# Forgetting attention's scores on a Trainium2 core: the order of 64-row products, 128-row bias products and one small copy

## Chip, core and metric

One NeuronCore of one Trainium2 chip runs the whole program. The metric is device time in microseconds (us) from one launch; three runs of the kernel before gave 2244.13, 2245.39 and 2246.12 us, so the median is 2245.39 us. Lower is better.

## What is computed

The reference runs two transformer blocks over 256 tokens of width 1024, each with attention to a 256-token memory and a mixture of experts. The second block begins with a hybrid mixer, and one of its three parts is the forgetting attention (4 heads of width 64), cut here to what matters:

```python
cum = jnp.cumsum(log_f, axis=-1)                     # log_f = log_sigmoid(ff + fox_fb), per head
logits = jnp.einsum('bhqd,bhkd->bhqk', q_blk, k).astype(jnp.float32) * scale
logits = logits + c_blk[..., :, None] - cum[..., None, :]
logits = jnp.where(key_pos[None, :] <= q_pos[:, None], logits, -jnp.inf)
p = jax.nn.softmax(logits, axis=-1).astype(v.dtype)
return jnp.einsum('bhqk,bhkd->bhqd', p, v)
```

## The kernel before

The kernel is written engine by engine, with semaphores set by hand, so that the order of the code is the order on each queue. TensorE (PE) does every product; VectorE (DVE) and ScalarE (ACT) split float32 weights into a high and a low part (`w_high`, `w_low`), and a product of weights is three matmuls (lines 809 to 811: high by high, low by high, high by low). ACT makes a high part (line 1449) and DVE the low part (`lows`, line 1923, one half-panel each); SyncE (SP) loads weight panels into three ring slots (line 469), and a slot is free when DVE has split its panel.

The mixer's projections stand on PE in the order `fqk` (queries and keys of the forgetting attention), `fv`, `hf`, `dqk`, `dv`, `hq`, `hi`, `hg`. After the first half of `hf` PE makes the running sums of the forget gates (`fox_sums`, lines 1179 to 1181), waits until DVE has copied them out of the PSUM bank that the scores will take (`small_read`, line 2566), and makes the scores (`fox_scores`). The second half of `hf`, the first half of `dqk`, and the turning of the probabilities (`turn_map(1)`, lines 1219 to 1221) follow.

A score tile is 128 queries by 128 keys (`tc` = 0, the first half of the queries) or by 256 keys (`tc` = 1). Per head it is a product of q by k over 64 rows of the array (line 1193 or 1197; rows 0 to 63 for heads 0 and 2, rows 64 to 127 for heads 1 and 3) and, accumulated onto it, the bias by products over all 128 rows: the log forget gates, broadcast, by a triangle of ones (`upto`) or by ones (line 1194, or lines 1198 to 1200). The heads go in the order 0, 2, 1, 3, and two heads share a PSUM bank: places 0 and 1 (heads 0 and 2) in bank 4 or 5, places 2 and 3 (heads 1 and 3) in bank 7 or 6. All these operands are float32, and each such matmul is two passes in the trace ("x2").

When a `tc` is done PE signals `map_scores`; DVE adds the query's own sum and the mask (line 2572), takes maxima (2002, 2003), splits the second half of `dqk` (1923), and normalises (2009, 2010) what ACT has exponentiated (1468). PE's `turn_map(1)` waits for that (`probs_ready`). The differential attention later makes its scores over 32 rows of the array in the same head order (line 1209), four 128-column and four 256-column products at a time with nothing between them; `diagonals` (line 1250) is eight 128-row, 128-column float32 products in a row.

Of the kernel before, what the change touches and what calls it, by code (L numbers as in the profile page):

```python
# [21 lines left out]
P = 128  # L22
T = 256
# [19 lines left out]
HEAD_ORDER = (0, 2, 1, 3)  # L43
# [155 lines left out]
def program(nc, ins, const_in, out):  # L199
    ctx = ExitStack()  # L200
    with ctx:
# [5 lines left out]
        def S(name):  # L207
            if name not in sems:
                sems[name] = ctx.enter_context(nc.semaphore(name))
            return sems[name]  # L210
# [21 lines left out]
        ps = ctx.enter_context(nc.psum_tensor("ps", [P, 8, 512], F32))  # L232

        def c_(name):

            a, n = CONST_COLS[name]
            if a >= RESIDENT:
                return ring[:, 6, a - RESIDENT:a - RESIDENT + n]
            return const[:, a:a + n]

        def w_(off, *shape):
            n = int(np.prod(shape))
            v = work[:, off:off + n]
            if len(shape) == 2:
                return v.rearrange("p (a b) -> p a b", b=shape[1])
            if len(shape) == 3:
                return v.rearrange("p (a b c) -> p a b c", b=shape[1], c=shape[2])
            return v
# [12 lines left out]
        def vec(name, r=0):  # L261
            a = VEC_AT[name] + r
            return cols[:, a:a + 1]

        IDENT, ONES = c_("ident"), c_("ones")
        FQK, DQK, QH, KH = w_(0, 4, T), w_(1024, 4, T), w_(2048, 4, T), w_(3072, 4, T)
# [69 lines left out]
        for u in range(len(UNITS) + 1):  # L336
# [15 lines left out]
            weight, layer, c0, n, columns, src = UNITS[u]  # L352
# [44 lines left out]
        def half_tile(q, parts):  # L397

            t, (_, kind, _, n) = parts[:, q % SPLITS, :], pieces_split[q]
            if kind == "rows":  # L400
                return t
            if kind == "features":
                return t.rearrange("p (k n) -> p k n", n=PANEL)[:, :, 0:n]
            if q in range(ffn_at, ffn_at + 3 * FFN_TURNS):
                return t.rearrange("p (k g n) -> p k g n", g=2, n=P)
            return t.rearrange("p (k n) -> p k n", n=T)

        def halves_to(name, more=0):

            return split_at[UNIT[name]] + 2 + more  # L410
# [222 lines left out]
        def _(pe):  # L633
            mm = nc.tensor.matmul
# [52 lines left out]
            def evicted(name):  # L687
                u = UNIT[name]
                pe.wait_ge(S(f"unit_read{u % 2}"), u // 2 + 1)
# [208 lines left out]
            for t in range(VEC_TILES):  # L898
                n = min(P, VEC_ROWS - t * P)
                last = nc.tensor.transpose(ps[:, 0, t * P:t * P + n], w_(0, VEC_TILES, P)[0:n, t, :], IDENT[0:n, 0:n])  # L900
# [7 lines left out]
            for g in range(4):  # L908
                last = mm(ps[:, 4 + g // 2, g % 2 * T:g % 2 * T + T], poolw[:, g, :], w_(0, 4, T)[:, g, :],
                          start=True, stop=True)  # L910
# [84 lines left out]
            for b in range(TAPS_ON_PE):  # L995
                for k in range(CONV):
# [3 lines left out]
                       start=(k == 0), stop=(k == CONV - 1)).then_inc(S("diagonal_used"), 1)  # L1000
# [7 lines left out]
            for kc in range(KC):  # L1008
# [4 lines left out]
                last = mm(ps[:, 7, 0:T], ONES, SQ[:, kc, :], start=(kc == 0), stop=(kc == KC - 1))  # L1013
# [161 lines left out]
            upto, ones = c_("upto"), ONES  # L1175
# [7 lines left out]
            def fox_scores():  # L1183

                evicted("fqk")
                for tc in range(2):
                    for place, h in enumerate(HEAD_ORDER):
                        p0 = 64 * (h % 2)
                        first, second = (minus_logf[:, i, h:h + 1].broadcast_to([P, P]) for i in range(2))
                        q = FQK[p0:p0 + 64, h // 2, tc * P:(tc + 1) * P]  # L1190
                        if tc == 0:
                            o = ps[:, 4 + 3 * (place // 2), place % 2 * P:place % 2 * P + P]
                            mm(o, q, FQK[p0:p0 + 64, 2 + h // 2, 0:P], start=True, stop=False)
                            last = mm(o, first, upto, start=False, stop=True)
                        else:
                            o = ps[:, 5 + place // 2, place % 2 * T:place % 2 * T + T]
                            mm(o, q, FQK[p0:p0 + 64, 2 + h // 2, :], start=True, stop=False)
                            mm(o[:, 0:P], first, upto, start=False, stop=False)
                            mm(o[:, P:T], first, ones, start=False, stop=False)
                            last = mm(o[:, P:T], second, upto, start=False, stop=True)  # L1200
                    last.then_inc(S("map_scores"), 1)

            def diff_scores(which):
# [121 lines left out]
            for h in range(4):  # L1325
# [3 lines left out]
                last = mm(ps[:, 5, h * P:(h + 1) * P], CR[:, h, :], v(0), start=False, stop=True)  # L1329
# [507 lines left out]
        def _(dve):  # L1837
# [80 lines left out]
            def lows(end):  # L1918

                while n_["halves"] < end:  # L1920
                    q = n_["halves"]
                    dve.wait_ge(S("parts_high"), q + 1)
                    V.tensor_tensor(half_tile(q, w_low), half_source(q), half_tile(q, w_high).bitcast(F32), SUB)\  # L1923
                        .then_inc(S("parts_split"), 1)
                    n_["halves"] += 1
# [38 lines left out]
            def row(b):  # L1964
                n_[f"b{b}"] += 1
                dve.wait_ge(S(f"brow{b}_loaded"), 16 * n_[f"b{b}"])
                return brow[:, b, :]
# [50 lines left out]
            def map_scores(tc):  # L2018
                if tc == 0:
                    return ps[:, 4:8:3, 0:T].rearrange("p a (b t) -> p a b t", t=P)  # L2020
                return ps[:, 5:7, :].rearrange("p a (b t) -> p a b t", t=T)
# [93 lines left out]
            for k in range(3):  # L2115
                for b in range(4):
                    wv = vec("ev_conv_a", 4 * k + b)
                    if k == 0:
                        last = V.tensor_scalar(CT[:, b, :], AP_[:, b, 0:T], wv, None, MUL)
                    else:  # L2120
                        last = V.scalar_tensor_tensor(CT[:, b, :], AP_[:, b, k:k + T], wv, CT[:, b, :], MUL, ADD)
# [4 lines left out]
            for g, win in enumerate(WINDOWS):  # L2126

                cur, size, nxt = UP[:, g, :], 1, SA
                while size < win:
                    n = 272 - 2 * size  # L2130
# [4 lines left out]
                last = V.tensor_tensor(PO[:, g, :], PO[:, g, :], UP[:, g, 8:264], SUB)  # L2135
# [9 lines left out]
            for g in range(4):  # L2145
                if g % 2 == 0:
                    n_["act"] += 1
                    dve.wait_ge(S("columns_by_act"), n_["act"])
                last = V.scalar_tensor_tensor(XT_low[:, 4 + g, :], ps[:, 4 + g // 2, g % 2 * T:g % 2 * T + T], vec("ev_pool_scale", g),
                                              XT_high[:, 4 + g, :].bitcast(F32), MUL, SUB)  # L2150
# [20 lines left out]
            for e, raw in ((8, router1), (16, router)):  # L2171
# [3 lines left out]
                last = V.tensor_tensor(both[:, :, e:2 * e], raw, both[:, :, 0:e].bitcast(F32), SUB)  # L2175
# [53 lines left out]
            for j in range(2):  # L2229
# [17 lines left out]
                for b in range(4):  # L2247
                    last = V.scalar_tensor_tensor(inner[:, b, :], inner[:, b, :], vec("od_pw1_b", 4 * j + b),
                                                  w_(2304, 4, T)[:, b, :], ADD, MUL)
# [6 lines left out]
            for k in range(CONV):  # L2256
                for kc in range(KC - TAPS_ON_PE):
                    wv = vec("od_dw_w", KC * k + kc)
                    if k == 0:
                        last = V.tensor_scalar(CO[:, kc, :], HC[:, kc, 0:T], wv, vec("od_dw_b", kc), MUL, ADD)  # L2260
                    else:
                        last = V.scalar_tensor_tensor(CO[:, kc, :], HC[:, kc, k:k + T], wv, CO[:, kc, :], MUL, ADD)  # L2262
# [17 lines left out]
            for kc in range(KC):  # L2280
# [3 lines left out]
                last = V.tensor_tensor(XT_low[:, kc, :], SQ[:, kc, :], XT_high[:, kc, :].bitcast(F32), SUB)  # L2284
# [3 lines left out]
            b = row(0)  # L2288
# [225 lines left out]
            for tc in range(2):  # L2514
                last = V.tensor_tensor_reduce(out=scaled[:, tc, :], in0=H[:, tc, :], in1=g, scale=1.0, scalar=0.0, op0=MUL, op1=ADD,
                                              accum_out=mean[:, tc:tc + 1])
# [8 lines left out]
            for tc in range(2):  # L2525
                last = V.scalar_tensor_tensor(centred[:, tc, :], scaled[:, tc, :], mean[:, tc:tc + 1], g, ADD, MUL)
# [5 lines left out]
            for tc in range(2):  # L2532
                last = V.scalar_tensor_tensor(H[:, tc, :], centred[:, tc, :], rstd[:, tc:tc + 1], w_(11264, D), MUL, ADD)
# [25 lines left out]
            dve.wait_ge(S("fox_logits"), 1)  # L2559
            step(V.tensor_tensor(logf_fox, logf_fox, ffa, SUB))  # L2560
            V.tensor_scalar(minus_logf, logf_fox, -1.0, None, MUL).then_inc(S("fox_log"), 1)
            lows(halves_to("dqk", -1))

            cs = ffa
            dve.wait_ge(S("fox_sums"), 1)
            V.tensor_copy(cs, ps[:, 7, 496:504].rearrange("p (a e) -> p a e", e=4)).then_inc(S("small_read"), 1)
            dve.wait_ge(S("small_read"), 1)
            masks = row(0).rearrange("p (k a t) -> p k a t", k=2, a=2)
            for tc in range(2):
                dve.wait_ge(S("map_scores"), tc + 1)  # L2570
                for place, h in enumerate(HEAD_ORDER):
                    last = V.scalar_tensor_tensor(MAPS[1][tc][:, place, :], map_scores(tc)[:, place // 2, place % 2, :], cs[:, tc, h:h + 1],
                                                  masks[:, 0, tc, 0:(tc + 1) * P], ADD, ADD)
# [39 lines left out]
            first, second = w_(8192, 12 * P), w_(9728, 12 * P)  # L2613
# [125 lines left out]
            for tc in range(2):  # L2739
                last = V.scalar_tensor_tensor(centred[:, tc, :], XS[:, tc, :], mean[:, tc:tc + 1], g, ADD, MUL)  # L2740
# [4 lines left out]
            b = row(1 - gain_row[0])  # L2745
# [27 lines left out]
```

## Time and profile before

| what | value |
|---|---|
| runs | 2244.13, 2245.39, 2246.12 us; median 2245.39 |
| profiled execution's own span | 2245.6 us |
| PE busy | 2184.1 us, 97% of the span |
| DVE busy | 1726.1 us, 77% |
| ACT busy | 1363.6 us, 61% |
| mean granted TensorE clock | 0.987 of full |

The page lists for each engine the time in which it was busy. A granted clock (PEclk) of 1.00 is 2.4 GHz, one of 0.50 is 1.2 GHz. The span is from the first instruction to the last of the one profiled execution; it is 0.2 us over the median of the runs.

### The profile page before, as it was taken

How to read it: one execution, taken by the hardware profiler on the slowest of the kernel's cores; microseconds unless marked ns; L12 is line 12 of the kernel's file. 1: busy time of each engine (PE TensorE's matmuls, PEld its weight loads, DVE VectorE, ACT ScalarE, POOL GpSimd, SP SyncE). 2: the span in 40 equal slices, each digit the busy share in tenths (PEclk: the TensorE clock that was granted, in tenths of full speed). 3: DMA queues.
4: the chain of work that ended last, by engine and by line, in shares of the span. 5: the costliest groups of instructions: out<-in, count | busy, mean ns of one | idle time of the engine just before them, and what ended most of it. 6: DMA issues, size and time to landing. Idle time of an engine off the chain costs nothing. (4 is left out here: it accounts for less than half of the span.)

```text
span 2245.6 us, 30564 instructions
## 1 busy us (share of the span) xinstructions
PE 2184.1 (97%) x11743; PEld 1872.3 (83%) x11743; DVE 1726.1 (77%) x1614; ACT 1363.6 (61%) x1205; POOL 83.4 (4%) x79
## 2 busy tenths in 40 slices
PE   7999999999999999999999999999899999999997
PEld 7998999968878888888888888888689988788886
DVE  4755555698568888888888888888756665698897
ACT  4454333427457777777777777777546344477775
POOL 3000000000000000000000000000000000000000
PEclk9999999999999999999999999999889999999999
DMA  9542555532279999999999999999634251799995
GB/s 301 186 160 94 193 200 193 183 113 82 78 282 383 375 386 376 380 375 382 375 381 380 375 390 367 383 366 396 254 130 160 76 200 63 247 365 380 375 379 228
DMA packets 274825, 617.26 MB, mean 275 GB/s; under 512 B 9537, under 2 KB 34321, under 8 KB 274737
## 3 DMA queue, kind: packets, MB, share of 16 engines
q1 hardware_dynamic: 265648, 584.43, 71.1%
q0 software_dynamic: 9088, 31.60, 4.6%
q8 instruction: 62, 1.02, 0.2%
q14 instruction: 27, 0.21, 0.0%
HBM read 603.41 MB, written 12.58 MB: 274 GB/s over the span
## 5 line engine op out<-in xcount | busy, mean ns | idle before, releaser
L2464 DVE TENSOR_TENSOR w_low<-ring,w_high 128x2048 fp32r<-128x2048 f32 x426 | 971.3, 2290 | 134.6 <-ACT w_high L1730 134.0
L1730 ACT ACTIVATE w_high<-ring 128x2048 fp32r<-128x2048 f32 x426 | 815.2, 1917 | 169.1 <-PE ps L811 169.1
L810 PE MATMUL ps<-w_high,parts 128*128 128x512 f32 (+2 forms) x1896 | 736.5, 388 | 0.0
L809 PE MATMUL ps<-w_high,parts 128*128 128x512 f32 x1560 | 617.8, 396 | 4.8 <-DVE gates L2368 3.4
L811 PE MATMUL ps<-w_low,parts 128*128 128x512 f32 x1560 | 609.0, 390 | 0.0
L810 PEld LDWEIGHTS ps<-w_high,parts 128*128 128x128 f32 x1896 | 357.5, 189 | 69.4
L1923 DVE TENSOR_TENSOR w_low<-ring,w_high 128x2048 fp32r<-128x2048 f32 (+2 forms) x117 | 262.2, 2253 | 115.2 <-ACT w_high L1449 109.0
L809 PEld LDWEIGHTS ps<-w_high,parts 128*128 128x128 f32 x1560 | 293.3, 188 | 66.7 <-DVE gates L2368 3.8
L811 PEld LDWEIGHTS ps<-w_low,parts 128*128 128x128 f32 x1560 | 293.3, 188 | 62.7
L1449 ACT ACTIVATE w_high<-ring 128x2048 fp32r<-128x2048 f32 (+2 forms) x117 | 219.7, 1884 | 147.3 <-PE ps L811 127.1
L809 PE MATMUL ps<-XT_high,w_high 128*128 128x256 f32 x1024 | 293.4, 287 | 7.0 <-DVE parts L1914 5.2
L810 PE MATMUL ps<-XT_high,w_low 128*128 128x256 f32 x1024 | 290.7, 284 | 0.0
L811 PE MATMUL ps<-parts,w_high 128*128 128x256 f32 x1024 | 290.6, 284 | 0.0
L809 PE MATMUL ps<-w_high,XT_high 128*128 128x512 f32 (+2 forms) x592 | 232.5, 393 | 2.7 <-DVE parts L2284 1.3
L811 PE MATMUL ps<-w_low,XT_high 128*128 128x512 f32 (+2 forms) x592 | 228.3, 386 | 0.0
L809 PEld LDWEIGHTS ps<-XT_high,w_high 128*128 128x128 f32 x1024 | 197.4, 193 | 10.7 <-issue 8.1
L810 PEld LDWEIGHTS ps<-XT_high,w_low 128*128 128x128 f32 x1024 | 197.4, 193 | 0.7
L811 PEld LDWEIGHTS ps<-parts,w_high 128*128 128x128 f32 x1024 | 197.4, 193 | 0.0
L809 PEld LDWEIGHTS ps<-w_high,XT_high 128*128 128x128 f32 x592 | 111.8, 189 | 25.6 <-issue 3.9
L811 PEld LDWEIGHTS ps<-w_low,XT_high 128*128 128x128 f32 x592 | 111.6, 189 | 22.8
L810 PE MATMUL ps<-w_high,XT_high 128*128 128x512 f32 x256 | 99.6, 389 | 0.0
L2262 DVE SCALAR_TENSOR_TENSOR work<-work,cols 128x256 f32<-128x256 f32 x180 | 74.0, 480 | 1.1
(445 smaller groups left out, 1661.7 us busy)
## 6 DMA issues: line engine op xcount, KB each, us to landing
ring<-in_od_moe_gu SPq DMA_DIRECT2D x224, 1024.0 KB, 8.2
ring<-in_od_moe_down SPq DMA_DIRECT2D x112, 1024.0 KB, 7.6
ring<-in_w SPq DMA_DIRECT2D x96, 1024.0 KB, 8.6
ring<-in_ev_ffn_gu SPq DMA_DIRECT2D x22, 1024.0 KB, 7.7
ring<-in_xa_wkv SPq DMA_DIRECT2D x8, 2048.0 KB, 8.2
ring<-in_od_pw_w SPq DMA_DIRECT2D x6, 2048.0 KB, 8.4
ring<-in_w_in SPq DMA_DIRECT2D x6, 2048.0 KB, 7.9
ring<-in_ev_ffn_down SPq DMA_DIRECT2D x11, 1024.0 KB, 5.1
```

The lines of the kernel that those rows point to most:

```text
L809: mm(out_, xh, wh, start=start, stop=False)
L810: mm(out_, xl, wh, start=False, stop=False)
L811: return mm(out_, xh, wl, start=False, stop=stop)
L1449: A(half_tile(q, w_high), half_source(q), ACT.Copy).then_inc(S("parts_high"), 1)
L1730: A(w_high[:, j % SPLITS, :], ring[:, j % NS, :], ACT.Copy).then_inc(moe_sem(k, "high"), 1)
L1923: V.tensor_tensor(half_tile(q, w_low), half_source(q), half_tile(q, w_high).bitcast(F32), SUB)\
L2262: last = V.scalar_tensor_tensor(CO[:, kc, :], HC[:, kc, k:k + T], wv, CO[:, kc, :], MUL, ADD)
L2464: V.tensor_tensor(w_low[:, j % SPLITS, :], ring[:, j % NS, :], w_high[:, j % SPLITS, :].bitcast(F32), SUB)\
```

## The change

In `fox_scores` the four 64-row products of a `tc` are issued together, and the 128-row bias products of all four heads behind them. A bank's first product carries `start`, the bank's second goes without it, and the checks on groups are skipped. On DVE the copy of the sums, with PE's permission that follows from it, stands ahead of the low part of `dqk`'s first half, no longer behind it. Numbers of instructions, their sizes and operands stay.

```diff
 evicted("fqk")
 for tc in range(2):
+    n = (tc + 1) * P
+    places = [ps[:, 4 + 3 * a if tc == 0 else 5 + a, b * n:(b + 1) * n] for a in range(2) for b in range(2)]
     for place, h in enumerate(HEAD_ORDER):
         p0 = 64 * (h % 2)
+        mm(places[place], FQK[p0:p0 + 64, h // 2, tc * P:(tc + 1) * P], FQK[p0:p0 + 64, 2 + h // 2, 0:n],
+           start=(place % 2 == 0), stop=False, skip_group_check=True)
+    for place, h in enumerate(HEAD_ORDER):
+        o = places[place]
         first, second = (minus_logf[:, i, h:h + 1].broadcast_to([P, P]) for i in range(2))
-        q = FQK[p0:p0 + 64, h // 2, tc * P:(tc + 1) * P]
-        if tc == 0:
-            o = ps[:, 4 + 3 * (place // 2), place % 2 * P:place % 2 * P + P]
-            mm(o, q, FQK[p0:p0 + 64, 2 + h // 2, 0:P], start=True, stop=False)
-            last = mm(o, first, upto, start=False, stop=True)
-        else:
-            o = ps[:, 5 + place // 2, place % 2 * T:place % 2 * T + T]
-            mm(o, q, FQK[p0:p0 + 64, 2 + h // 2, :], start=True, stop=False)
-            mm(o[:, 0:P], first, upto, start=False, stop=False)
-            mm(o[:, P:T], first, ones, start=False, stop=False)
-            last = mm(o[:, P:T], second, upto, start=False, stop=True)
+        last = mm(o[:, 0:P], first, upto, start=False, stop=(tc == 0), skip_group_check=True)
+        if tc == 1:
+            mm(o[:, P:T], first, ones, start=False, stop=False, skip_group_check=True)
+            last = mm(o[:, P:T], second, upto, start=False, stop=True, skip_group_check=True)
     last.then_inc(S("map_scores"), 1)
...
 V.tensor_scalar(minus_logf, logf_fox, -1.0, None, MUL).then_inc(S("fox_log"), 1)
-lows(halves_to("dqk", -1))

 cs = ffa
 dve.wait_ge(S("fox_sums"), 1)
 V.tensor_copy(cs, ps[:, 7, 496:504].rearrange("p (a e) -> p a e", e=4)).then_inc(S("small_read"), 1)
 dve.wait_ge(S("small_read"), 1)
+lows(halves_to("dqk", -1))
```

PE before, from the last of the sums through the scores of `tc` = 0 and one head of `tc` = 1 (the second matmul operand's columns close each row):

```order
L1181 MATMUL ps<-small,const 128x4
L1193 MATMUL ps<-work 128x128 [waits unit_read0,small_read]
L1194 MATMUL ps<-const,small 128x128
L1193 MATMUL ps<-work 128x128
L1194 MATMUL ps<-const,small 128x128
...
L1197 MATMUL ps<-work 128x256
L1198 MATMUL ps<-const,small 128x128
L1199 MATMUL ps<-const,small 128x128
L1200 MATMUL ps<-const,small 128x128
L1197 MATMUL ps<-work 128x256
```

The same place on PE with the change (L1191 is the 64-row product, L1196 to L1199 the bias; the rows of the last three heads' bias, which repeat these, are left out):

```order
L1181 MATMUL ps<-small,const 128x4
L1191 MATMUL ps<-work 128x128 [waits unit_read0,small_read]
L1191 MATMUL ps<-work 128x128 x3
L1196 MATMUL ps<-const,small 128x128 x4
L1191 MATMUL ps<-work 128x256 x4
L1196 MATMUL ps<-const,small 128x128
L1198 MATMUL ps<-const,small 128x128
L1199 MATMUL ps<-const,small 128x128
```

Before, each head changes from 64 rows to 128 rows and back; with the change there are one block of 64-row and one of 128-row products for each `tc`.

DVE before, from the gates' logarithms to the first additions onto the scores:

```order
L2561 TENSOR_SCALAR small<-small 128x8 [waits vector_step]
L1923 TENSOR_TENSOR w_low<-ring,w_high 128x2048 [waits parts_high]
L2566 COPY small<-ps 128x8 [waits fox_sums]
L2572 SCALAR_TENSOR_TENSOR work<-ps,small,brow 128x128 [waits map_scores,brow0_loaded,small_read]
L2572 SCALAR_TENSOR_TENSOR work<-ps,small,brow 128x128 x3
```

DVE with the change, same place:

```order
L2560 TENSOR_SCALAR small<-small 128x8 [waits vector_step]
L2564 COPY small<-ps 128x8 [waits fox_sums]
L1922 TENSOR_TENSOR w_low<-ring,w_high 128x2048 [waits parts_high,small_read]
L2571 SCALAR_TENSOR_TENSOR work<-ps,small,brow 128x128 [waits map_scores,brow0_loaded]
L2571 SCALAR_TENSOR_TENSOR work<-ps,small,brow 128x128 x3
```

The copy has moved ahead of one low part, which is now held until the sums are there.

## Rows read from the trace of the kernel before

**Rows 1.** The page's busy times, shares of the span.

```profile
PE 2184.1 (97%) x11743; PEld 1872.3 (83%) x11743; DVE 1726.1 (77%) x1614; ACT 1363.6 (61%) x1205; POOL 83.4 (4%) x79
```

**Rows 2.** PE's waits from 1700 us to the end; total us, times, longest.

```profile
PE ps L809 <- DVE gates L2368: 1.8, 1, 1.8
...
PE ps L674 <- DVE XS L2688: 0.4, 1, 0.4
PE ps L1105 <- DVE XS L2410: 0.3, 1, 0.3
```

**Rows 3.** PE's timeline at the scores: start us, us, instruction, [idle before <-releaser].

```profile
1661.73 0.36 PE L1181 MATMUL ps<-small,const 128*128 128x4 f32 x2
1663.33 0.48 PE L1193 MATMUL ps<-work 64*128 64x128 f32 x2 [1.23 <-DVE small L2566]
1663.75 0.49 PE L1194 MATMUL ps<-const,small 128*128 128x128 f32 x2
...
1666.06 0.79 PE L1193 MATMUL ps<-work 64*128 64x128 f32 x2
1666.79 0.79 PE L1194 MATMUL ps<-const,small 128*128 128x128 f32 x2
...
1669.25 0.63 PE L1199 MATMUL ps<-const,small 128*128 128x128 f32 x2
1669.67 0.63 PE L1200 MATMUL ps<-const,small 128*128 128x128 f32 x2
...
1678.14 0.77 PE L809 MATMUL ps<-w_high,XT_high 128*128 128x512 f32 x1
```

**Rows 4.** PE's timeline at line 1250, eight 128-row float32 products in a row.

```profile
1728.69 2.02 PE L1250 MATMUL ps<-work 128*128 128x128 f32 x16
1730.47 0.48 PE L809 MATMUL ps<-w_high,XT_high 128*128 128x512 f32 x1
```

**Rows 5.** Busy us and granted clock (PEclk) of stretches around the scores.

```profile
1661.40:1665.50 4.10, 2.87 (x18) 2.17 (x16) 1.88 (x2) 3.19 (x2) 0.00 (x0) 1.00 1.03 393
1668.60:1678.10 9.50, 9.50 (x31) 6.82 (x31) 0.24 (x1) 0.00 (x0) 0.00 (x0) 0.50 0.00 0
1678.10:1682.60 4.50, 4.50 (x13) 3.53 (x13) 3.90 (x9) 1.38 (x7) 0.00 (x0) 0.50 0.00 0
1682.60:1685.80 3.20, 3.20 (x16) 2.61 (x15) 3.06 (x5) 2.24 (x10) 0.00 (x0) 1.00 0.05 3
```

**Rows 6.** PE's timeline: start and end of `hf`'s first half, end of its second.

```profile
1655.89 0.40 PE L809 MATMUL ps<-w_high,XT_high 128*128 128x512 f32 x1
...
1661.37 0.28 PE L1179 MATMUL ps<-small,const 128*128 128x4 f32 x2
...
1685.79 0.28 PE L809 MATMUL ps<-XT_high,w_high 128*128 128x256 f32 x1
```

**Rows 7.** DVE's timeline from the log gates to the first additions.

```profile
1659.37 0.17 DVE L2561 TENSOR_SCALAR small<-small 128x8 f32<-128x8 f32 x1
1660.91 2.29 DVE L1923 TENSOR_TENSOR w_low<-ring,w_high 128x2048 fp32r<-128x2048 f32 x1 [1.37 <-ACT w_high L1449]
1663.12 0.16 DVE L2566 COPY small<-ps 128x8 f32<-128x8 f32 x1
1667.72 1.12 DVE L2572 SCALAR_TENSOR_TENSOR work<-ps,small,brow 128x128 f32<-128x128 f32 x4 [4.44 <-PE ps L1194]
```

**Rows 8.** PE's timeline at line 1209, 32-row products of the differential attention.

```profile
1715.51 1.68 PE L1209 MATMUL ps<-work 32*128 32x128 f32 x16
1717.12 0.38 PE L809 MATMUL ps<-XT_high,w_high 128*128 128x256 f32 x1
```

**Rows 9.** Timeline behind the scores: DVE's additions and normalising, PE's turning.

```profile
1678.60 1.66 DVE L2572 SCALAR_TENSOR_TENSOR work<-ps,small,brow 128x256 f32<-128x256 f32 x4 [9.75 <-PE ps L1200]
...
1685.71 1.22 DVE L2010 TENSOR_TENSOR work<-work,small 128x1024 f32<-128x1024 f32 x1
...
1691.55 0.27 PE L1219 MATMUL ps<-const,work 128*128 128x128 f32 x1
```

**Rows 10.** Other stretches: busy us of PE, PEld, DVE, ACT, POOL, then PEclk.

```profile
1774.80:1778.20 3.40, 2.14 (x20) 2.00 (x19) 3.37 (x5) 3.35 (x4) 0.00 (x0) 0.99 0.02 5
1778.20:1785.00 6.80, 6.80 (x34) 6.80 (x34) 5.60 (x9) 1.06 (x2) 0.00 (x0) 0.50 0.07 8
1787.80:1791.90 4.10, 2.90 (x18) 2.39 (x18) 2.68 (x6) 1.21 (x4) 0.00 (x0) 1.00 0.69 260
1955.70:1959.10 3.40, 3.40 (x9) 2.64 (x8) 0.78 (x2) 0.50 (x1) 1.84 (x1) 0.50 1.04 364
```

## The prediction

> **What bounds the kernel now.** I read the page's busy times first: PE is busy for 97% of the span and DVE for 77% [rows 1], so the question is what PE loses at the place of the change, and whether a gain there is kept. The waits of PE behind that place come next: the list has ten kinds, none on a DMA, the longest 1.8 us, and all on DVE or ACT work that PE itself feeds [rows 2]. So PE sets the end, and what it gains at the scores should arrive at the end nearly whole.
>
> Then PE's timeline at the scores. The reader is to see three losses. PE stands idle for 1.23 us before the first product, until DVE's copy [rows 3]. Then a 64-row product and a 128-row product alternate, start to start 0.42 us, where eight 128-row products of that size without such a change take 1.78 us, 0.22 us each [rows 3, 4]. And the spacing grows: from 1666.06 it is 0.73 us for the same alternation, because the granted clock, 1.00 up to about 1665.5, is 0.50 (1.2 GHz instead of 2.4) from there to 1682.6, past the end of the scores and well into `hf`'s second half [rows 3, 5]. The scores take from 1663.33 to 1678.14, 14.81 us [rows 3], and `hf`'s second half from there to 1685.79, 7.65 us, where its first half, as large, took 5.48 us from 1655.89 to 1661.37 [rows 3, 6].
>
> **The wait for the copy.** DVE has nothing to do from 1659.54 to 1660.91, then makes `dqk`'s low part for 2.29 us, and copies the sums only at 1663.12 [rows 7]; PE had them ready at 1661.73 + 0.36 = 1662.09 [rows 3]. With the copy first, DVE starts it 0.14 us after PE's end (as at line 2572: 1666.79 + 0.79 = 1667.58, started 1667.72 [rows 3, 7]), takes 0.16, and PE starts 0.05 later (1663.28 to 1663.33). That is 1662.44: a gain of **0.9 us**. The low part then runs from about 1662.4 to 1664.7 where it ended at 1663.2. It is queued ahead of the additions of `tc` = 0, which could start at about 1664.2, so these are held by 0.5 us; the additions of `tc` = 1 wait for PE till after 1668 in any case. PE needs that low part only when `dqk` begins, behind all of `hf`. So moving it costs nothing. If the cover went, it would cost at most those 0.5 us.
>
> **The changes between 64 and 128 rows.** A change costs 0.42 - 0.22 = 0.20 us at full clock, and 0.73 - 0.42 = 0.31 at half, the 0.42 being lines 1199 to 1200 at half clock [rows 3, 4]. Among the scores there are 15 such changes, 7 within each `tc` and one between; with the edit 3 are left. Twelve go: **2.4 us** at full clock.
>
> **The 64-row products side by side.** No row shows 64-row products in sequence. The nearest is line 1209: four 128-column and four 256-column products over 32 rows, same head order, same banks. Its 16 passes and the change to what follows take 1717.12 - 1715.51 = 1.61 us [rows 8]. One behind another they would take 4 x 0.22 + 4 x 0.43 = 2.6 us and 0.2 for the change, so half of them ran beside the others: two heads lie in one part of the array's rows and two in another. The forgetting heads lie likewise in rows 0 to 63 and 64 to 127, and the two parts write different banks. The bounds are no pairing (2.6 us, gain nothing) and full pairing (1.4 us): **1.2 us**, of which I take all, by that row.
>
> **The clock.** The scores after, at full clock: 1.61 for the 64-row blocks, 16 bias products at 0.22 = 3.56, two more changes 0.4: 5.6 us. The scores before would be 2.6 + 3.56 + 15 x 0.20 = 9.2 us at full clock, against 14.8 measured; so the low clock costs 5.6 us there, and 7.65 - 5.48 = 2.2 us in `hf`: 7.8 us in all. Does it still fall? Before it fell, PE was busy for 2.87 of 4.10 us, and most products had a change ahead of them [rows 5]. The busy share alone does not tell: PE was busy for 2.90 of 4.10 us at 1787.8 and the clock stayed at 1.00, and it fell after 2.14 of 3.40 us at 1774.8 [rows 10]. The same stretch of the changed kernel has 0.35 us of idle time (1662.09 to 1662.44) and two changes, so some 0.9 busy; that lies on the side of the stretches that kept it. I take the clock as held: **7.8 us**, bounds 0 and 7.8.
>
> The Trainium skill has a rule on weight loads that speaks against packing the bias products: by "TensorE: Matmul & The Clock Gate", Part 3, The mechanism, a weight load overlaps running matmuls only when the row group differs, which would leave every pass of a block of 128-row products with its load in the open. The trace does not bear it out: 16 passes, each with its own load, started in 1.78 us [rows 4].
>
> **The sum.** 0.9 + 2.4 + 1.2 + 7.8 = 12.3 us. Checked the other way: from 1662.44, 5.6 for the scores and 5.5 for `hf`'s second half end at 1673.5 instead of 1685.79. Downstream, DVE's chain from the additions of `tc` = 1 to the normalised maps took from 1678.60 to 1686.93 = 8.3 us, and PE turned them at 1691.55, 4.6 us later [rows 9]. After: scores done 1668.0, chain done 1676.5, PE there at 1668.0 + 5.5 + 5.76 (`dqk`, 1685.79 to 1691.55) = 1679.3; 2.8 us to spare. What is late next is this chain, not yet binding. Profiled span 2245.6 - 12.3 = 2233.3; the span stands 0.2 over the median of the runs, so **2233.1 us**.
>
> **Rivals.** *The clock falls all the same* (0.19). It is the largest term, and other stretches show it falls at shares not far off [rows 10]. If it fell at 1665.5 as before, 2.5 us of full-clock work would take 5, and `hf` would lose up to the 2.2 us that it loses now: 4.7 us given back, 2237.8. The short low stretches elsewhere, 3.4 and 6.8 us [rows 10], would cost half their length, 1.7 or 3.4. I put this case at 2236.0.
>
> *The 64-row products run one behind another* (0.05): the edit then saves only changes, and 1.2 us stay: 2234.3. Against it: the 32-row products [rows 8]; for it: these were 32 rows, not 64.
>
> *Weight loads of the bias products in the open* (0.02): every one of 32 passes costs about 0.21 us, as a first pass after a change does, not 0.11: 3.2 us back, 2236.3. This is the rule of the page named above, and the block of 128-row products is against it [rows 4].
>
> *The chain on DVE and ACT takes over* (0.04): the turning waits for the probabilities. It decides once the chain is 2.8 us later than worked out; a chain as long as the 4.4 us wait it would replace gives 2235 to 2237. For it: DVE now makes a low part between sums and additions. Against: DVE waited 4.44 and 9.75 us for PE there [rows 7, 9].
>
> *Slower* (0.02): the block of 64-row products leaves the clock low, and `hf` and `dqk` do not bring it back. Low clock costs half of its length, so the gains of 12.3 us are gone once it is low for some 25 us from 1662.4, to about 1687 on the new time axis, beyond the turning; each further 2 us costs 1, and low until 1693 gives 2248. Against it: full-size products brought the clock back within 4.5 us here [rows 5].
>
> **How the numbers follow.** About 0.2% (4.5 us) is what a measurement of this kernel can tell from no change. The forecast has 0.68. All cases but the last, and a small part of the clock and chain cases together (0.03), gain over 4.5 us: faster 0.95, same 0.03, slower 0.02. The range takes the forecast's own scatter, since other low stretches later (3.4 and 6.8 us [rows 10]) can shrink, go or grow as PE arrives earlier, 1.7 us each way for one: 2230.5 at the low end. The high end takes in no pairing and all but the worst of the fallen clock: 2237.5.
>
> **What would show each step.** Right: PE's wait before line 1191 about 0.3 us; 16 passes of line 1191 in pairs; a gap of 0.2 us at only three changes; PEclk 1.00 from 1662 through `hf`; first `dqk` product near 1673.5; `turn_map` without a wait. Wrong: PEclk 0.50 anywhere between 1665 and 1675, spacing of 0.21 us and not 0.11 between passes of line 1191 or 1196, or a wait of line 1219 on DVE line 2009.

## The result and the profile after

The changed kernel took 2231.59 to 2233.53 us in four runs, median **2232.7**, against 2242.99 to 2246.12 us, median 2244.76, for the kernel before beside it: a ratio of 0.9946 with a 95% interval of 0.9934 to 0.9958, some 12 us. The forecast was 2233.1 us, in a range of 2230.5 to 2237.5. One run below, of the kernel with the wait filled, was in a slow state (2429.9 us, granted clock 0.849) and enters no figure.

The page's busy times, as [rows 1]: PE is busy for 13.9 us less, the other engines for as long as before.

```profile
span 2230.7 us, 30565 instructions
PE 2170.2 (97%) x11743; PEld 1862.7 (84%) x11743; DVE 1726.2 (77%) x1614; ACT 1363.5 (61%) x1205; POOL 81.5 (4%) x79
```

PE's timeline at the scores of the changed kernel (start us, us, instruction, idle before it and its releaser), which answers to [rows 3]:

```profile
1661.93 0.28 PE L1179 MATMUL ps<-small,const 128*128 128x4 f32 x2
...
1662.29 0.36 PE L1181 MATMUL ps<-small,const 128*128 128x4 f32 x2
1662.91 0.72 PE L1191 MATMUL ps<-work 64*128 64x128 f32 x8 [0.26 <-DVE small L2564]
1663.56 1.16 PE L1196 MATMUL ps<-const,small 128*128 128x128 f32 x8
1664.65 1.14 PE L1191 MATMUL ps<-work 64*128 64x256 f32 x8
1665.72 0.49 PE L1196 MATMUL ps<-const,small 128*128 128x128 f32 x2
1666.04 0.39 PE L1198 MATMUL ps<-const,small 128*128 128x128 f32 x2
...
1668.42 0.48 PE L809 MATMUL ps<-w_high,XT_high 128*128 128x512 f32 x1
...
1673.98 0.28 PE L809 MATMUL ps<-XT_high,w_high 128*128 128x256 f32 x1
```

Four blocks, three changes of rows, and a short wait in front. The scores take 1668.42 - 1662.91 = 5.51 us instead of 14.81, and `hf`'s second half 5.56 instead of 7.65. Because the whole program may run a little earlier or later in a given execution, the best measure is the stretch from the start of `hf`'s first half (1656.45 here, 1655.89 before [rows 6]) to the first product of `dqk`: 17.53 us against 29.90, **12.37 us less**.

The stretches of the changed kernel (busy us of PE, PEld, DVE, ACT, POOL, then PEclk), as [rows 5]:

```profile
1661.30:1664.70 3.40, 3.14 (x28) 2.70 (x26) 1.98 (x2) 2.63 (x3) 0.00 (x0) 1.00 0.95 342
1664.70:1668.40 3.70, 3.70 (x33) 3.34 (x33) 1.52 (x5) 0.70 (x1) 0.00 (x0) 1.00 0.64 249
1668.40:1674.00 5.60, 5.60 (x28) 4.63 (x27) 5.12 (x9) 2.61 (x13) 0.00 (x0) 1.00 0.00 0
```

The granted clock is 1.00 all the way, where it was 0.50 for 17 us.

DVE's timeline, and the turning on PE, as [rows 7] and [rows 9]:

```profile
1662.69 0.17 DVE L2564 COPY small<-ps 128x8 f32<-128x8 f32 x1 [2.59 <-PE ps L1181]
1662.89 2.29 DVE L1922 TENSOR_TENSOR w_low<-ring,w_high 128x2048 fp32r<-128x2048 f32 x1
1665.10 1.12 DVE L2571 SCALAR_TENSOR_TENSOR work<-ps,small,brow 128x128 f32<-128x128 f32 x4
1668.77 1.66 DVE L2571 SCALAR_TENSOR_TENSOR work<-ps,small,brow 128x256 f32<-128x256 f32 x4 [2.55 <-PE ps L1199]
...
1675.89 1.23 DVE L2009 TENSOR_TENSOR work<-work,small 128x1024 f32<-128x1024 f32 x1
...
1679.74 0.27 PE L1218 MATMUL ps<-const,work 128*128 128x128 f32 x1
```

The low part stands right before the additions of the first half of the queries, without idle time between: it holds them by a fraction of a microsecond. The additions of the second half still wait for PE, the chain ends at 1675.89 + 1.23 = 1677.1, and PE turns the maps at 1679.74 without a wait, 2.6 us later (4.6 before).

Outside this place the two profiled executions differ by low stretches of clock that come and go. By the starts of like instructions behind each, the first puts the changed kernel back by 1.4 us, the second puts it ahead by 1.6 and the third by 1.3; another low stretch, between 1610 and 1630 us, puts it ahead by 0.8. They are no part of the 12.37 us. Before, then after:

```profile
640.00:650.00 10.00, 9.39 (x69) 8.98 (x69) 7.90 (x46) 7.08 (x10) 0.00 (x0) 0.83 1.04 403
1760.00:1790.00 30.00, 27.63 (x217) 27.25 (x215) 23.22 (x33) 13.72 (x15) 0.00 (x0) 0.89 0.19 65
1950.00:1965.00 15.00, 13.23 (x62) 10.98 (x62) 9.51 (x15) 8.55 (x10) 1.84 (x1) 0.89 0.88 260
```

```profile
640.00:650.00 10.00, 9.49 (x56) 9.12 (x57) 6.56 (x39) 6.40 (x8) 0.00 (x0) 0.66 1.04 405
1760.00:1790.00 30.00, 27.16 (x171) 24.42 (x171) 24.04 (x37) 11.68 (x18) 0.71 (x1) 0.94 0.24 85
1950.00:1965.00 15.00, 15.00 (x68) 11.99 (x67) 14.29 (x12) 11.26 (x8) 0.00 (x0) 1.00 1.03 354
```

With the 12.37 us they make up the difference of the two spans, 14.9 us, to 0.2 us; that of the medians is 12.1.

### The profile page after: what moved, and what is told of

It reads as the page before. It is cut to its first block and busy times, and to the rows that moved or that the text cites. A ratio compares the mean times of both kernels' runs of the same rounds, so it can differ in the third digit from the quotient of the medians.

```text
span 2230.7 us, 30565 instructions
## 1 busy us (share of the span) xinstructions
PE 2170.2 (97%) x11743; PEld 1862.7 (84%) x11743; DVE 1726.2 (77%) x1614; ACT 1363.5 (61%) x1205; POOL 81.5 (4%) x79
## 5 line engine op out<-in xcount | busy, mean ns | idle before, releaser
L1704 ACT ACTIVATE work<-ps 128x512 f32<-128x512 f32 x72 | 43.1, 598 | 52.0 <-PE ps L811 52.0
```

Of the source, the lines that this page charges most:

```text
L1704: A(SG, ps[:, 0, :], ACT.Silu).then_inc(moe_sem(k, "silu"), 1)
```

## The experiments

The prediction named four terms: the wait, the changes of rows, the pairing, and the clock, the largest. Open were what made the clock fall, the 1.23 us of idle time or the changes of rows, and whether each term has its size by itself. All ratios below are against the kernel before, run beside the kernel in question. Its medians were 2244.37 us beside the copy alone, the blocks alone, the heads apart and all scores first; 2244.48 beside the filled wait, all rows, rows 0 to 63 alone and the sums in `hf`; 2245.53 beside the last two fillings. A ratio is given with its 95% interval and can lie up to 0.0006 from the quotient of two medians. Each kernel has one trace, of one of its runs; what is said below of the clock is read from that trace, and for the other runs it is at most inferred from their times.

### Each half of the change alone

The copy ahead, the scores in their old order:

```diff
-lows(halves_to("dqk", -1))
 cs = ffa
 ...
 dve.wait_ge(S("small_read"), 1)
+lows(halves_to("dqk", -1))
```

> The copy of the sums is moved ahead of the low part, the scores stay in the old alternating order. Both theories: PE's wait falls from 1.23 to about 0.3 us, 15 changes stay at 0.20 us each at full clock. Idle theory (the 1.23 us of idle time brought the clock down): clock held, gain 0.9 + 7.8 = 8.7 us against the kernel before, scores 9.2 us long. Alternation theory (the changes between 64 and 128 rows brought it down): clock 0.50 again through most of the scores, gain 0.9 us alone, scores 13 to 15 us long.

Measured: median 2244.64 us, ratio 0.9995 (0.9981 to 1.0009). Its PE timeline and two stretches:

```profile
1662.80 0.48 PE L1193 MATMUL ps<-work 64*128 64x128 f32 x2 [0.26 <-DVE small L2565]
1663.21 0.49 PE L1194 MATMUL ps<-const,small 128*128 128x128 f32 x2
...
1676.76 0.77 PE L809 MATMUL ps<-w_high,XT_high 128*128 128x512 f32 x1
```

```profile
1661.30:1664.70 3.40, 3.14 (x19) 2.46 (x18) 2.09 (x2) 2.63 (x3) 0.00 (x0) 1.00 1.00 357
1668.10:1673.00 4.90, 4.90 (x15) 3.15 (x15) 0.00 (x0) 0.00 (x0) 0.00 (x0) 0.50 0.01 3
```

The wait is 0.26 us, and the clock falls all the same; the scores take 13.96 us. Note the first of the two stretches: PE was busy for 3.14 of 3.40 us there, exactly as in the changed kernel, where the clock did not fall. In the 3.40 us that end where it fell, from 1662.70 to 1666.10, PE was busy for 3.30, against 3.19 in the same stretch of the changed kernel. PE's busy share is no guide here. But the ten runs fall into two groups: eight lie between 2241.88 and 2248.26 us, with mean granted clocks of 0.987 to 0.990, two at 2235.22 and 2236.88, with 0.994 and 0.992. So, by the times, the low clock is not certain with this order. With the wait of 1.23 us none of the kernel before's 37 runs took less than 2242.20 us, which speaks for a low clock in all of them; one of them has a trace.

The blocks alone, the copy where it was (against the changed kernel):

```diff
+lows(halves_to("dqk", -1))
 cs = ffa
 ...
 dve.wait_ge(S("small_read"), 1)
-lows(halves_to("dqk", -1))
```

> The blocks of the change, but the copy behind the low part as before, so that PE stands idle for 1.23 us. Idle theory: the clock falls at about 1665.5 and comes back some time in hf; the gain is 2.4 + 1.2 and what shorter work at half clock saves, about 6 us against the kernel before. Alternation theory: clock held, gain 11.4 us against before, 0.9 us slower than the changed kernel.

Measured: median 2234.32 us, ratio 0.9960 (0.9946 to 0.9974). In its profile the wait is 1.23 us and the clock is low, but briefly; the row by itself shows its clock, 0.50, and behind 1667.6 us it is at full again:

```profile
1663.11 0.72 PE L1191 MATMUL ps<-work 64*128 64x128 f32 x8 [1.23 <-DVE small L2565]
1663.76 1.69 PE L1196 MATMUL ps<-const,small 128*128 128x128 f32 x8
1665.38 2.09 PE L1191 MATMUL ps<-work 64*128 64x256 f32 x8
1667.40 0.58 PE L1196 MATMUL ps<-const,small 128*128 128x128 f32 x2
...
1670.19 0.47 PE L809 MATMUL ps<-w_high,XT_high 128*128 128x512 f32 x1
```

```profile
1664.30:1667.50 3.20, 3.20 (x15) 2.17 (x14) 1.12 (x4) 0.32 (x1) 0.00 (x0) 0.50 0.59 228
```

The blocks in the middle take 1.69 and 2.09 us instead of 1.16 and 1.14, and `hf` is at full speed. Neither theory was right as it stood. The blocks bring most of the gain, 29.90 - 20.08 = 9.82 of the 12.37 us in the profile, where the clock is back after some 3.4 us; with the open wait it still fell for that long.

### The gap filled

If a gap and the changes are both needed, filling the gap with products must keep the clock even in the old order.

```diff
 fox_sums()
+keep_busy(12, 6)
 pe.wait_ge(S("small_read"), 1)
 fox_scores()
```

`keep_busy(12, 6)` is 12 transposes of the identity, 128 by 128, into a bank that nobody reads before the scores overwrite it.

> The kernel before with 12 full-size transposes (1.3 us) put into PE's wait for the copy; the scores keep the alternating order. If the idle time before the scores brought the clock down: clock held, gain 7.8 us against before. If the changes do it by themselves, with or without idle time: the clock falls in most runs all the same, gain near 0; as with the copy moved alone, one run in some can keep it and be 8 us faster.

Measured: median 2237.75 us over four runs, ratio 0.9966 (0.9952 to 0.9981), and 2236.97 us at the lowest. The profile is of the slowest of the four, 2240.67 us:

```profile
1662.96 1.51 PE L685 MATMUL ps<-const 128*128 128x128 f32 x12
1664.40 0.48 PE L1193 MATMUL ps<-work 64*128 64x128 f32 x2
1664.81 0.49 PE L1194 MATMUL ps<-const,small 128*128 128x128 f32 x2
...
1673.52 0.48 PE L809 MATMUL ps<-w_high,XT_high 128*128 128x512 f32 x1
```

The old order runs at full clock for 9.12 us from start to end: fifteen changes by themselves did not lower it. (What this run lost on its fellows it lost elsewhere: its granted clock is 0.66 from 640 to 650 us and 0.83 from 1765 to 1785.) Against 14.81 us this also measures the clock's share at the scores, 5.69 us.

The same with the copy ahead, where only 0.6 us are left from the last sum to the first score (`keep_busy(5, 6)` added to the run of the copy alone), and with the blocks and the late copy (`keep_busy(12, 6)` added to the run of the blocks alone):

> The copy moved ahead, alternating scores, and 5 full-size transposes (0.55 us) in what is left of PE's gap before the scores. With the copy ahead alone the clock fell in 8 of 10 runs. If the fall needs both the gap and the changes: clock held in all runs, scores 9.1 us as with the wait filled, from hf's first half to dqk 21.2 us, 2235.7 us. If the changes do it by themselves and the filled wait held it by chance: clock low again in most runs, about 2244.

> Blocks, the copy behind the low part, and 12 full-size transposes in the 1.23 us wait. The profile of blocks with that wait open showed the clock low for 3.4 us. If the gap made that: clock held, scores 5.5 us, from hf's first half to dqk 18.6 us (17.5 of the changed kernel, 1.0 for the later copy), 2233.7. Rival: still low for a while, 19 to 20 us.

Measured: 2235.62 us, ratio 0.9954 (0.9938 to 0.9971), and 2233.34 us, ratio 0.9948 (0.9932 to 0.9965). The first:

```profile
1661.98 0.36 PE L1181 MATMUL ps<-small,const 128*128 128x4 f32 x2
1662.21 0.74 PE L685 MATMUL ps<-const 128*128 128x128 f32 x5
```

The first score starts at 1662.88, without idle time. All four runs lie between 2235.4 and 2236.77 us; the scores take 9.12 us. Five transposes that compute nothing, in a gap of 0.6 us, are worth 9 us in the median against the same kernel without them. At this place the two profiles show 27.35 - 21.40 = 5.95 us of it; the rest lies elsewhere, part of it in a low stretch (a granted clock of 0.83 from 1770 to 1790 us with the copy alone, 1.00 from 1760 to 1790 with the gap filled), and no experiment says whether the transposes have to do with that. The blocks with the wait filled take 5.51 us, as in the changed kernel, with the clock held in the profile; one of the four runs took 2236.94 us, 3.6 over their median, and has no trace. So with the changes in the old order it was what is left of the gap that decided whether the clock fell.

### What a change of rows costs

```diff
-q = FQK[p0:p0 + 64, h // 2, tc * P:(tc + 1) * P]
+q = FQK[:, h // 2, tc * P:(tc + 1) * P]
...
-mm(o, q, FQK[p0:p0 + 64, 2 + h // 2, 0:P], start=True, stop=False)
+mm(o, q, FQK[:, 2 + h // 2, 0:P], start=True, stop=False)
```

> The kernel before, same order and same number of products, but the q by k products run over all 128 rows instead of 64 (they then sum two heads, so this computes other scores). No product changes the number of rows, none can be paired. If the price lies in the change of rows: spacing 0.22 us instead of 0.42 in the first half of the queries, scores 6.2 us long after a 1.23 us wait, clock held or low for a few us at most, gain 9 to 11 us against before. If it lies in the alternation of operands, or in accumulating onto a tile that was just written: spacing 0.42 stays and nothing is gained.

Measured: median 2234.16 us, ratio 0.9953 (0.9938 to 0.9969).

```profile
1662.58 0.49 PE L1193 MATMUL ps<-work 128*128 128x128 f32 x2 [1.23 <-DVE small L2566]
1662.91 0.39 PE L1194 MATMUL ps<-const,small 128*128 128x128 f32 x2
1663.13 0.39 PE L1193 MATMUL ps<-work 128*128 128x128 f32 x2
1663.35 0.39 PE L1194 MATMUL ps<-const,small 128*128 128x128 f32 x2
...
1668.80 0.48 PE L809 MATMUL ps<-w_high,XT_high 128*128 128x512 f32 x1
```

```profile
1661.30:1664.70 3.40, 2.17 (x19) 2.10 (x19) 1.23 (x2) 2.78 (x2) 0.00 (x0) 1.00 1.05 397
```

Same order, same accumulation onto the tile just written, and the spacing is 0.22 us. The price comes with the change in the number of rows, not with the order or the accumulation. Scores 6.21 us; with the filled wait and 64 rows 9.12: 15 changes cost 2.91 us, **0.19 us each**. And with the 1.23 us wait left open the clock stays at full here, after the same 2.17 busy us of 3.40 as in the blocks alone, and all four runs lie between 2232.98 and 2235.13 us: the wait alone did not bring it down either. One caution: the q by k products of this kernel use twice the rows, and the transposes of the filled kernels are added work. Whether the gap and the changes count as such, or only how much PE gets done around them, these runs don't separate.

### What pairing is worth

Two kernels take the pairing away: one issues heads 0 and 2 with their bias ahead of heads 1 and 3, the other lets all four heads' products read rows 0 to 63.

```diff
+for two in (range(0, 2), range(2, 4)):
-    for place, h in enumerate(HEAD_ORDER):
+    for place, h in ((p, HEAD_ORDER[p]) for p in two):
...
-    for place, h in enumerate(HEAD_ORDER):
+    for place, h in ((p, HEAD_ORDER[p]) for p in two):
...
```

> The changed kernel, but heads 0 and 2 get their 64-row products and their bias before heads 1 and 3 get theirs: 7 changes instead of 3, and the two halves of the array's rows are never in use together. Pairing theory: a block of two 64-row products (4 passes) takes as long as the changed kernel's block of four (8 passes), 0.65 us for 128 columns; scores longer by 4 x 0.20 + 1.2 = 2.0 us, 7.5 us in all. If pairing were worth nothing: longer by 0.8 us alone. If the clock falls it shows as 0.50 and more than 3 us.

```diff
-p0 = 64 * (h % 2)
+p0 = 0
```

> The changed kernel with the 64-row products of heads 1 and 3 reading rows 0 to 63 too (so that those two heads get the scores of heads 0 and 2). Blocks, changes and sizes stay; no two products can run side by side. Pairing theory: block of the first half 1.1 us instead of 0.65, of the second 1.9 instead of 1.07, scores 1.2 us longer than the changed kernel's 5.5; clock held. If pairing does not come from the two halves of the rows: no difference.

Measured: 2236.07 us, ratio 0.9967 (0.9954 to 0.9979), and 2235.55 us, ratio 0.9957 (0.9942 to 0.9972), the clock held at this place in both profiles. Heads apart, then rows 0 to 63 alone:

```profile
1662.16 0.71 PE L1192 MATMUL ps<-work 64*128 64x128 f32 x4 [0.26 <-DVE small L2565]
1662.80 0.71 PE L1197 MATMUL ps<-const,small 128*128 128x128 f32 x4
```

```profile
1662.40 1.16 PE L1191 MATMUL ps<-work 64*128 64x128 f32 x8 [0.26 <-DVE small L2564]
1663.49 1.16 PE L1196 MATMUL ps<-const,small 128*128 128x128 f32 x8
1664.58 1.99 PE L1191 MATMUL ps<-work 64*128 64x256 f32 x8
1666.50 0.49 PE L1196 MATMUL ps<-const,small 128*128 128x128 f32 x2
```

Four passes of two heads take 0.64 us with the change behind them, just what eight passes of four heads take in the changed kernel (0.65); and when all eight passes use rows 0 to 63 they take 1.09, and 1.92 for 256 columns instead of 1.07. The scores are 7.57 and 6.79 us long against 5.51, so pairing is worth **1.28 us**. The two kernels agree: four more changes at 0.19 and the lost pairing on top of 5.51 make 7.55 us, against 7.57 for the heads apart. And from the filled wait to rows 0 to 63 alone only twelve changes go, 9.12 - 6.79 = 2.33 us, again 0.19 each. (Two of the six runs of the heads apart took 2238.5 and 2238.9 us; the profile is of the fastest, 2234.14, so whether the clock held in those two is not known.)

### Further in the same direction

All eight 64-row products first, one change of rows instead of three:

```diff
 for tc in range(2):
     for place, h in enumerate(HEAD_ORDER):
         p0 = 64 * (h % 2)
...
+for tc in range(2):
     for place, h in enumerate(HEAD_ORDER):
+        o = places(tc)[place]
...
```

> All eight 64-row products of both halves of the queries first, then all 16 bias products: one change instead of three. Cost of changes at 0.20 us each: scores 5.1 us instead of 5.5, 0.4 us less than the changed kernel, the additions of the first half of the queries start 1 us later and nobody waits for them. Rival: the later additions hold the chain, and turn_map waits.

And on top of it, the sums two products of weights ahead of the end of `hf`'s first half:

```diff
-project("hf", halves=(0,))
-fox_sums()
+project("hf", halves=(0,), inside=fox_sums)
...
+if inside and tc == 1 and k == 2:
+    inside()
```

> All eight 64-row products first (as in the run of that kind), and the three sums of the gates are issued two blocks before the end of hf's first half, so that DVE copies them while PE still multiplies. PE's gap from the last sum to the first score, 0.6 us in the changed kernel, goes; with the two changes saved 0.9 to 1.0 us less than the changed kernel, 2231.7. Rival: the logarithms are not ready so early (they were 1.8 us before the end of hf's first half) and PE waits inside hf for what it saves.

Measured: 2232.56 us, ratio 0.9949 (0.9932 to 0.9966), and 2233.06 us, ratio 0.9945 (0.9932 to 0.9959). Neither can be told from the changed kernel by its time. By the profile the stretch from `hf` to `dqk` is 17.22 and 17.02 us against 17.53: the first saves 0.31 where 0.4 was expected, the second 0.5 where 0.9 to 1.0 was. The later additions held nobody: PE turns the maps 5.75 us after the start of `dqk`, as before. Inside `hf` the sums still take PE's time, 0.59 us from 1660.51 to 1661.10, and the product behind them 0.1 us more than its like, so that only 0.2 us of the gap goes:

```profile
1660.51 0.28 PE L1181 MATMUL ps<-small,const 128*128 128x4 f32 x2
...
1660.87 0.36 PE L1183 MATMUL ps<-small,const 128*128 128x4 f32 x2
1661.10 0.48 PE L811 MATMUL ps<-w_high,XT_high 128*128 128x512 f32 x1
1661.41 0.40 PE L812 MATMUL ps<-w_high,parts 128*128 128x512 f32 x1
```

### All runs, by the stretch from `hf` to `dqk` in their profiles

| kernel | sums and wait: `hf` to scores | scores | `hf`, second half | sum |
|---|---|---|---|---|
| before | 7.44 | 14.81 | 7.65 | 29.90 |
| copy ahead alone | 6.46 | 13.96 | 6.92 | 27.35 |
| wait filled | 7.50 | 9.12 | 5.57 | 22.19 |
| copy ahead, gap filled | 6.74 | 9.12 | 5.55 | 21.40 |
| blocks alone | 7.43 | 7.08 | 5.57 | 20.08 |
| heads apart | 6.46 | 7.57 | 5.57 | 19.60 |
| all rows, alternating | 7.43 | 6.21 | 5.55 | 19.20 |
| rows 0 to 63 alone | 6.46 | 6.79 | 5.55 | 18.81 |
| blocks, wait filled | 7.50 | 5.51 | 5.55 | 18.56 |
| changed kernel | 6.46 | 5.51 | 5.56 | 17.53 |
| all scores first | 6.46 | 5.20 | 5.55 | 17.22 |
| and sums in `hf` | 6.26 | 5.21 | 5.56 | 17.02 |

## Why the prediction was right

**The wait.** Forecast 0.9 us, measured 7.44 - 6.46 = 0.98. The copy started 0.04 us behind PE's end (1662.69 after 1662.29 + 0.36), where 0.14 was taken. The low part's move cost nothing, as forecast.

**The changes.** Forecast 12 at 0.20, 2.4 us. Measured 0.19 each, 2.3 us.

**The pairing.** Forecast 1.2 us, measured 1.28. The reading of the 32-row products [rows 8] carried over to 64 rows, and the three terms leave the blocks at 5.51 us, forecast 5.6. The unpaired order was a rival at 0.05, and the two kernels without pairing show what it would have been: 1.3 us.

**The clock.** Forecast 7.8 us, measured 14.81 - 9.12 = 5.69 at the scores and 7.65 - 5.56 = 2.09 in `hf`, 7.8 us. The size was worked out soundly. The forecast that the clock would be held came true in the profile, and no run of the changed kernel was slow enough for a long fall. But the reason given was weak, so this term, nearly two thirds of the sum, came out right partly by luck. The prediction looked at PE's busy share, 0.9 against 0.7; the copy alone had the same 0.9 and, by its times, lost the clock in eight of ten runs, while the all-rows kernel had the low share and kept it. What the share could not tell, the filled waits and the all-rows kernel show: a gap of 0.6 to 1.2 us followed by fifteen changes of rows brought it down; fifteen changes without a gap, or the gap without changes, did not; the gap with three changes did for 3.4 us, and 0.6 us with three changes, which is the changed kernel, did not. The rival of the fallen clock lived in a milder form in the blocks alone, a fall that cost 1.6 us of the scores (7.08 against 5.51). The price of 4.7 us was not seen with blocks.

**Weight loads in the open.** Refuted: the bias block of 24 passes from 1665.72 to 1668.42 takes 2.70 us, 0.11 a pass after the first. The Trainium skill's sentence in "TensorE: Matmul & The Clock Gate", Part 3, The mechanism, that a weight load overlaps running matmuls only when the row group differs, does not hold for a stream of full 128-row products here. The same section also lets a load run ahead into a background weight buffer, which the prediction left out and which would agree with these passes; no run here shows the buffer itself.

**The chain and the end.** The room before the turning was forecast at 2.8 us and is 2.6. The prediction put the end of the chain 8.5 us behind the scores (1668.0 to 1676.5), with 0.2 us from PE's last product to the additions; it is 1668.42 to 1677.12, 8.7, with 0.35 us there. PE's waits behind 1700 us are the same ten in the changed kernel, to 0.1 us, so the local 12.37 us arrived whole; the medians moved by 12.1, with an interval of 9.4 to 14.8 us by the ratio's.

**The base.** One step was loose: the text put the profiled span 0.2 us over the median. In every later run the device time is 1.8 us more than the span, so the profiled execution of before took some 2247.4 us, 2 over the median. It did no harm, because 12.3 taken from the median of 2245.4 is the 2233.1 that was given.

## What to carry to other kernels

Products over fewer than 128 rows of the array, float32 here, should be issued next to each other, both halves of the rows together, and never in turn with full-height ones: each change of height cost 0.19 us, and the lost pairing as much as the paired products themselves (1.09 us instead of 0.65 with the change behind them, 1.92 instead of 1.07). A short gap in front of alternating work can halve the clock for many times its own length (here 17 us behind a gap of 1.23); look at the granted clock before costing a gap by its idle time, and move or fill the gap. When two faults together trip the clock, an experiment that removes one can show nothing or everything, so take both away, one at a time and together.

## What was not expected

- The copy alone was worth 2.55 us from `hf` to `dqk` in its profile, 0.98 of it the wait, and nothing in the median, yet five empty transposes behind it made 9 us. Transposes of the identity were enough to keep the clock up.
- The kernel with the copy alone had two outcomes, 2235 to 2237 us in two runs and 2242 to 2248 in eight, with nothing changed between them.
- PE's busy share was 3.14 of 3.40 us around the start of the scores both where the clock fell and where it held.
- Why the gap and the changes tripped the clock only together was not settled; the runs show the combinations, not the rule behind them, and not whether a gap filled with other work than transposes would do.
